# First attention's query and key products as matmul pairs over both halves of x, in two banks a panel

## The chip, the cores and the metric

The kernel runs on one core of one Trainium2 chip. The metric is the device time of one execution in microseconds; lower is better. All arithmetic is in fp32, with TensorE working on operands of type fp32r, so each large product is made of three: high half times high half, low times high, high times low.

## The reference

Two transformer blocks in a row work on `x` of 256 tokens by 1024. The first projects the normalised x to all its inputs at once, runs two mixers side by side, and adds a feed-forward network. The part that matters here is the first mixer, an attention with a forget gate:

```python
hn = rmsnorm(h, norm_mix[l])
proj = jnp.einsum('bsd,de->bse', hn, w_in[l])
(fq, fk, fv, ff, gq, gk, gv, ga, gb, gz, gate_fox, gate_gdn) = split_in(proj)
y_fox = fox_attention(fq.reshape(B, S, 8, 128), fk..., fv..., log_f)   # 8 heads
# in fox_attention, for each head and block of 128 queries:
s = jnp.einsum('bhqd,bhkd->bhqk', qi, kh) * 128 ** -0.5 + (ci[..., :, None] - c[..., None, :])
p = softmax(where(causal, s, -inf));  o = p @ vh
```

The other mixer is a chunked gated delta rule; in the stage of interest it needs the inverse of sixteen 128 x 128 lower triangular matrices. Then come gates, branch and output projections, the feed-forward networks, and the second block.

## The kernel before

**Steps.** All large products run as 252 steps, in one order written out in `panels()`. A panel is 1024 rows of a weight matrix by 256 columns (1 MB); a step multiplies half of one panel (`HALVES`), four rows-of-128 blocks `k`. `END[key]` is the last step of a product. Five programs run side by side, one for each engine, and each walks through `for n in range(1, STEPS + 1)` and does at step n what is written under it, strictly in that order. TensorE first does `gemm(n)`, then the small products of step n. ScalarE (`scalar_program`) and VectorE (`vector_program`) each begin step n with `split(n + 3)`: ScalarE rounds the raw panel to its high half (`panel_hi`, L1090, once TensorE has finished step n - 1), and VectorE subtracts it from the raw panel for the low half (`panel_lo`, L1586). SyncE fetches the panels (L2394) as VectorE sets raw buffers free.

**Forms of a product.** `gemm` (L584 is where every matmul is recorded) has three forms. "fm": weights are the stationary operand and 256 tokens of x stream by; three matmuls of 256 columns for each k and column tile j, and both column tiles lie in one bank of PSUM. "hl": the weights' high half meets both halves of x in one matmul of 512 columns, and their low half meets the high half of x in one of 256; a column tile then fills a whole bank, with high sums in columns 0 to 255 and low ones in 256 to 511, which are to be added afterwards. "wide": x is stationary. The convolution products (steps 5 to 32, but for z) and six of eight branch products are "hl" already. In the convolution stage they use three banks in turn (4, 0, 1), and the helpers' bank ring `side` is cut from four banks to three (5, 6, 7).

**Queries and keys.** Steps 41 to 56 make the first attention's queries and keys: panels fq0, fk0, fq1, fk1, ..., fk3, two steps each, in form "fm". Each fills one bank; `fox_project` on ScalarE, near the end of its program for the panel's last step, waits for that step's last matmul and copies the bank, scaled for queries, into two heads of `qfT` or `kfT`.

**What else runs at steps 40 to 60.** The attention takes one head every three steps: for head hh with F = 45 + 3 hh, TensorE makes the scores (L897 is the transpose, `fox_scores` uses `mm`) at the end of step F, VectorE adds the bias at F + 1 (L1830), ScalarE takes the exponential at F + 2 (L1259) and loads the next head's bias, VectorE normalises at F + 3 (L1838, L1841), and TensorE turns the tile at F + 4 (L897) and multiplies by the values at F + 5. Beside it VectorE inverts the diagonal 16 x 16 blocks row by row at steps 42 to 47 (L1757, L1760). SyncE writes the result to memory at step 48 (L2440, L2442) and reads it back into `X` and `XT` (L2448), which TensorE uses from the end of step 53 on. ScalarE zeroes `X` at step 42 and `XT` at step 44.

Of the kernel before, what the change touches and what calls it, by code (L numbers as in the profile page):

```python
# [23 lines left out]
P = 128  # L24
T = 256
# [66 lines left out]
def panels():  # L92
# [20 lines left out]
    for j in range(4):  # L113
        for kind, c0 in (("fq", C_FQ), ("fk", C_FK)):
            add((kind, j), "mix", True, "w_in", 0, KD, c0 + j * PW)
# [54 lines left out]
SQUARED_K = [c for c in SQUARED if CONVS[c][0] == "k"]  # L170
FOX_AT = {45 + 3 * hh: hh for hh in range(HEADS)}
# [31 lines left out]
def build(nc, a, out, scratch_a, scratch_x, scratch_c):  # L203
    ctx = ExitStack()
    with ctx:
# [29 lines left out]
        X = at("X", [P, UNITS, 64], 17)  # L235
        XT = at("XT", [P, UNITS, P], 18)
# [208 lines left out]
        s_yf_hi = sem("yf_hi")  # L445
        s_gate_f, s_gate_g, s_mixed, s_y_hi, s_y = (sem(n) for n in ("gate_f_affine", "gate_g_affine", "mixed", "y_hi",
# [18 lines left out]
        rings = {"few": [0, 1], "conv": [4, 0, 1], "fox": [2, 3], "side": [4, 5, 6, 7], "gemm": [0, 1, 2, 3]}  # L465
# [46 lines left out]
        def ring_of(key):  # L512
            if key[0] == "z" or key in (("fv", 0), ("fq", 0), ("fk", 0)):
                return "fox"
            if key in CONVS and CONVS.index(key) in CONV_BOTH:
                return "conv"
            return "few" if END[key] <= END["gate_g", 3] else "gemm"
# [64 lines left out]
        def tensor_program(e):  # L582
# [297 lines left out]
            def fox_scores(hh):  # L880
# [4 lines left out]
                e.wait_ge(*emptied(("fq", hh // 2)))  # L885
                e.wait_ge(*emptied(("fk", hh // 2)))
# [112 lines left out]
            for n in range(1, STEPS + 1):  # L999
# [3 lines left out]
                if n == END["v", 3] + 2:  # L1003
                    rings["side"] = [4, 5, 6, 7]
# [83 lines left out]
        def scalar_program(e):  # L1088
# [184 lines left out]
            def fox_project(kind, j):  # L1273
                e.wait_ge(*product((kind, j)))
                dst, scale = (qfT, float(DH) ** -0.5) if kind == "fq" else (kfT, 1.0)
                copy(dst[:, 2 * j:2 * j + 2, :], pairs(bank_of((kind, j))), scale).then_inc(empties((kind, j)), 1)
# [123 lines left out]
            for n in range(1, STEPS + 1):  # L1400
                split(n + 3)
                if n == 13:
# [99 lines left out]
                for j in range(4):  # L1502
                    for kind in ("fq", "fk"):
                        if n == END[kind, j]:
                            fox_project(kind, j)
# [72 lines left out]
        def vector_program(e):  # L1578
# [242 lines left out]

            def fox_bias(hh):
# [223 lines left out]
            for n in range(1, STEPS + 1):  # L2046
                split(n + 3)
                if n == 13:
# [135 lines left out]
                if n == 76:  # L2184
                    for b in range(4):
                        hi, lo = (y_[:, 2 * b:2 * b + 2, :].rearrange("p h (t q) -> p (h t) q", t=2)
                                  for y_ in (ygh, ygl))
                        e.wait_ge(s_yg_hi, b + 1)
                        e.scalar_tensor_tensor(lo, units(bank_of(("yg", b))), PR("gdn_norm"), hi.bitcast(F32), ALU.mult,
                                               ALU.subtract).then_inc(empties(("yg", b)), 1)  # L2190
                if n - 5 in FOX_AT:
# [362 lines left out]
```

## Time and profile before

| | us |
|---|---|
| median of 3 runs | 806.5 (806.42 to 807.1) |
| the profiled execution | 806.4 |
| its span | 805.1 |
| TensorE busy | 798.8 (99%) |
| VectorE busy | 599.7 (74%) |
| ScalarE busy | 451.0 (56%) |
| GpSimd busy | 73.8 (9%) |
| matmul instructions | 5448 |

Matmul records overlap, since they are pipelined: the time that one costs is the distance from its start to the start of the next. "PE" is TensorE, "PEld" its weight loads, "DVE" VectorE, "ACT" ScalarE, "POOL" GpSimd, "SPq" SyncE's queue. A few matmul records are missing in places, so distances are read from first to last start.

### The profile page before, as it was taken

What the parts mean: (1) busy time and instruction counts of PE and PEld (TensorE: products, weight loads), DVE (VectorE), ACT (ScalarE), POOL (GpSimd) and SP (SyncE); (2) the same over time, 40 slices, a digit from 0 to 9 for tenths busy, and PEclk for the clock granted to TensorE, in tenths of its full rate; (3) what the DMA queues carried; (4) which work ended last, traced back from release to release, by engine and by line L of the source; (5) the groups of instructions that cost most, each with busy time, mean ns of one, the idle gap of its engine ahead of it and who ended that gap; (6) DMA issues with size and microseconds to landing.
All of it is one profiled execution on the core that took longest, in us unless ns stands there. A gap on an engine that the chain in (4) does not pass through costs nothing.

```text
span 805.1 us, 13705 instructions
## 1 busy us (share of the span) xinstructions
PE 798.8 (99%) x5448; PEld 712.3 (88%) x5448; DVE 599.7 (74%) x1021; ACT 451.0 (56%) x739; POOL 73.8 (9%) x65
## 2 busy tenths in 40 slices
PE   8999999999999999999999999999999999999998
PEld 6888888999999989899999998887878888888887
DVE  6889998875554776769999996486766777778543
ACT  6667677454535554546656564366665655655441
POOL 0001000010011203001101110021100111011000
PEclk9999999999999999999999999999999999999999
DMA  8755564647442544575687665555425656656641
GB/s 262 239 173 160 179 229 148 173 108 223 125 116 90 178 162 161 204 242 179 198 248 244 213 204 194 178 183 171 144 82 168 203 177 208 191 177 207 191 154 73
DMA packets 126255, 144.12 MB, mean 179 GB/s; under 512 B 11488, under 2 KB 103024, under 8 KB 125936
## 3 DMA queue, kind: packets, MB, share of 16 engines
q1 hardware_dynamic: 123744, 141.22, 55.2%
q10 hardware_dynamic: 2448, 2.03, 0.9%
q8 instruction: 43, 0.70, 0.4%
q14 instruction: 20, 0.16, 0.1%
HBM read 141.78 MB, written 1.46 MB: 178 GB/s over the span
## 4 chain that ended last, share of the span: by engine, by line
PE 96%; DVE 2%; DMA 1%; ACT 0%; issue 0%; POOL 0%; SPq 0%; DVEq 0%; ACTq 0%
PE bank L584 93%; PE bank L638 1%; DMA panel_raw<-in_w_in 1%; DVE conv_acc L1622 1%; PE bank L948 0%; PE bank L670 0%; DVE panel_lo L1586 0%; PE bank L897 0%; PE bank L921 0%; PE bank L725 0%; DVE x_halves L1607 0%; POOL stats L2301 0%; ACT x_halves L1090 0%; DVE norm_gained L1881 0%; PE bank L827 0%
## 5 line engine op out<-in xcount | busy, mean ns | idle before, releaser
L584 PE MATMUL bank<-x_halves,panel_hi 128*128 128x256 f32 (+1 forms) x1792 | 415.1, 317 | 0.7 <-DVE x_halves L2032 0.7
L1586 DVE TENSOR_TENSOR panel_lo<-panel_raw,panel_hi 128x1024 fp32r<-128x1024 f32 x251 | 313.8, 1253 | 134.5 <-ACT panel_hi L1090 133.8
L1090 ACT ACTIVATE panel_hi<-panel_raw 128x1024 fp32r<-128x1024 f32 (+1 forms) x253 | 266.3, 1055 | 164.6 <-PE bank L584 160.4
L584 PE MATMUL bank<-x_halves,panel_lo 128*128 128x256 f32 x1152 | 324.4, 282 | 0.0
L584 PEld LDWEIGHTS bank<-x_halves,panel_hi 128*128 128x128 f32 x1792 | 295.8, 190 | 23.5 <-issue 0.9
L584 PEld LDWEIGHTS bank<-x_halves,panel_lo 128*128 128x128 f32 x1152 | 219.4, 190 | 0.2
L584 PE MATMUL bank<-panel_hi,x_halves 128*128 128x512 f32 x256 | 80.6, 396 | 0.2 <-DVE panel_lo L1586 0.2
L584 PE MATMUL bank<-panel_hi,act_hi 128*128 128x512 f32 x176 | 68.6, 390 | 0.0
L584 PE MATMUL bank<-panel_hi,act_lo 128*128 128x512 f32 x176 | 68.5, 389 | 0.0
L584 PE MATMUL bank<-panel_lo,act_hi 128*128 128x512 f32 x176 | 68.5, 389 | 0.0
L584 PEld LDWEIGHTS bank<-panel_hi,x_halves 128*128 128x128 f32 x256 | 46.7, 188 | 10.4 <-DVE panel_lo L1586 1.0
L584 PE MATMUL bank<-panel_lo,x_halves 128*128 128x512 f32 x128 | 50.0, 391 | 0.0
L584 PEld LDWEIGHTS bank<-panel_hi,act_hi 128*128 128x128 f32 x176 | 33.0, 188 | 6.9
L584 PEld LDWEIGHTS bank<-panel_lo,act_hi 128*128 128x128 f32 x176 | 33.0, 188 | 6.8
L584 PEld LDWEIGHTS bank<-panel_hi,act_lo 128*128 128x128 f32 x176 | 33.0, 188 | 6.7
L2301 POOL TENSOR_TENSOR stats<-stats 128x2 f32<-128x2 f32 (+1 forms) x9 | 17.1, 1899 | 183.9 <-DVE stats L1600 102.6
L1622 DVE SCALAR_TENSOR_TENSOR conv_acc<-conv_tmp,params,conv_acc 128x255 f32<-128x255 f32 (+2 forms) x72 | 30.4, 477 | 1.4 <-ACT conv_acc L1090 1.4
L584 PEld LDWEIGHTS bank<-panel_lo,x_halves 128*128 128x128 f32 x128 | 24.0, 188 | 5.3
L2326 POOL TENSOR_TENSOR ff_tanh<-ff_tanh,ff_val 128x512 f32<-128x512 f32 x11 | 17.2, 1564 | 112.4 <-DVE ff_tanh L1929 112.4
L2306 POOL TENSOR_TENSOR key_bias<-key_bias,constants 128x128 f32<-128x128 f32 x16 | 8.5, 550 | 176.9 <-DMA key_bias<-gate_sums 176.9
L2333 POOL TENSOR_TENSOR f_tanh<-f_tanh,ff_val 128x512 f32<-128x512 f32 x11 | 14.3, 1301 | 108.3 <-DVE f_tanh L2005 108.3
L584 PE MATMUL bank<-yf_halves,panel_hi 128*128 128x512 f32 (+1 forms) x80 | 22.7, 350 | 0.0
(291 smaller groups left out, 936.6 us busy)
## 6 DMA issues: line engine op xcount, KB each, us to landing
panel_raw<-in_w_in SPq DMA_DIRECT2D x38, 1024.0 KB, 5.3
panel_raw<-in_w_up SPq DMA_DIRECT2D x30, 1024.0 KB, 5.3
panel_raw<-in_w_down SPq DMA_DIRECT2D x20, 1024.0 KB, 5.1
panel_raw<-in_w_gate SPq DMA_DIRECT2D x10, 1024.0 KB, 5.3
panel_raw<-in_w_out SPq DMA_DIRECT2D x8, 1024.0 KB, 5.0
panel_raw<-in_w_in SPq DMA_DIRECT2D x11, 512.0 KB, 4.6
panel_raw<-in_w_branch_fox SPq DMA_DIRECT2D x4, 1024.0 KB, 5.1
panel_raw<-in_w_branch_gdn SPq DMA_DIRECT2D x4, 1024.0 KB, 5.3
```

The lines of the kernel that those rows point to most:

```text
L584: return e.matmul(o, l, r, start=start, stop=stop, skip_group_check=True)
L638: i_ = e.transpose(b3[:, k, m * P:(m + 1) * P], h[:, m, f * P:(f + 1) * P], ident)
L1090: return e.activation(o, i_, ACT.Copy, scale=scale)
L1586: e.tensor_tensor(lo, raw_view(i, k0, kt), hi.bitcast(F32), ALU.subtract).then_inc(s_lo, 1)
L1622: e.scalar_tensor_tensor(acc[:, f, back:], tmp[:, f, 0:T - back], gconv(p, f, back), acc[:, f, back:], ALU.mult, ALU.add).then_inc(s_taps, 1)
L2301: return e.tensor_tensor(cols, cols, minus_half.broadcast_to([P, n]), ALU.pow)
L2306: i_ = e.tensor_tensor(key_bias[:, s], key_bias[:, s], C("causal"), ALU.add)
L2326: e.tensor_tensor(th, th, ff_acc[j % 2][1], ALU.mult).then_inc(s_f_mul, 1)
L2333: e.tensor_tensor(th, th, ff_acc[j % 2][1], ALU.mult).then_inc(s_g_mul, 1)
```

## The change

The eight panels of queries and keys take the form "hl". They use the ring of three banks (4, 0, 1), two banks for each panel, and the side ring is cut to 5, 6, 7 from step 41 until step 58. ScalarE copies the low sums of both column tiles (256 columns each) to one of two new tiles at the front of its program for the panel's last step; the second copy waits for that step's last matmul. VectorE multiplies the high sums by the scale and adds the copy: for the first column tile at the front of its program for that step, for the second after that step's other duties, ahead of the attention's. `fox_project` is gone. `fox_scores` waits for the one tile that it reads.

```diff
-            add((kind, j), "mix", True, "w_in", 0, KD, c0 + j * PW)
+            out.append(((kind, j), "mix", "hl", "w_in", 0, KD, c0 + j * PW, PW))
...
+FQK = [(kind, j) for j in range(4) for kind in ("fq", "fk")]
...
+        fqk_low = [at(f"fqk_low{i}", [P, 2, T], 17.5, skip=2048 * i) for i in range(2)]
...
-        rings = {"few": [0, 1], "conv": [4, 0, 1], "fox": [2, 3], "side": [4, 5, 6, 7], "gemm": [0, 1, 2, 3]}
+        rings = {"few": [0, 1], "fqk": [4, 0, 1], "conv": [4, 0, 1], "fox": [2, 3], "side": [4, 5, 6, 7], "gemm": [0, 1, 2, 3]}
...
         def ring_of(key):
-            if key[0] == "z" or key in (("fv", 0), ("fq", 0), ("fk", 0)):
+            if key[0] == "z" or key == ("fv", 0):
                 return "fox"
+            if key in FQK:
+                return "fqk"
...
-                e.wait_ge(*emptied(("fq", hh // 2)))
-                e.wait_ge(*emptied(("fk", hh // 2)))
+                e.wait_ge(*emptied(("fq", hh // 2, hh % 2)))
+                e.wait_ge(*emptied(("fk", hh // 2, hh % 2)))
...
+                if n == FIRST_HALF["fq", 0] + 1:
+                    rings["side"] = [5, 6, 7]
+                if n == END["fk", 3] + 2:
+                    rings["side"] = [4, 5, 6, 7]
                 gemm(n)
...
-            def fox_project(kind, j):
-                e.wait_ge(*product((kind, j)))
-                dst, scale = (qfT, float(DH) ** -0.5) if kind == "fq" else (kfT, 1.0)
-                copy(dst[:, 2 * j:2 * j + 2, :], pairs(bank_of((kind, j))), scale).then_inc(empties((kind, j)), 1)
+            def fqk_low_copy(kind, j):
+                p = FQK.index((kind, j))
+                for m in range(2):
+                    if p >= 2:
+                        e.wait_ge(*emptied((*FQK[p - 2], m)))
+                    e.wait_ge(*product_of((kind, j), m))
+                    copy(fqk_low[p % 2][:, m, :], bank_of((kind, j, m))[:, T:2 * T],
+                         float(DH) ** -0.5 if kind == "fq" else 1.0).then_inc(s_fqk_low, 1)
...
             for n in range(1, STEPS + 1):
                 split(n + 3)
+                for kind, j in FQK:
+                    if n == END[kind, j]:
+                        fqk_low_copy(kind, j)
...
+            def fqk_sum(kind, j, m):
+                p = FQK.index((kind, j))
+                dst, scale = (qfT, float(DH) ** -0.5) if kind == "fq" else (kfT, 1.0)
+                e.wait_ge(s_fqk_low, 2 * p + m + 1)
+                e.scalar_tensor_tensor(dst[:, 2 * j + m, :], bank_of((kind, j, m))[:, 0:T], scale,
+                                       fqk_low[p % 2][:, m, :], ALU.mult, ALU.add).then_inc(empties((kind, j, m)), 1)
...
             for n in range(1, STEPS + 1):
                 split(n + 3)
+                for kind, j in FQK:
+                    if n == END[kind, j]:
+                        fqk_sum(kind, j, 0)
...
+                for kind, j in FQK:
+                    if n == END[kind, j]:
+                        fqk_sum(kind, j, 1)
                 if n - 5 in FOX_AT:
                     fox_lo(FOX_AT[n - 5])
```

## Rows read from the trace of the kernel before

**Rows 1.** The page: busy us (share) xinstructions; tenths in 40 slices; the chain's shares.

```profile
PE 798.8 (99%) x5448; PEld 712.3 (88%) x5448; DVE 599.7 (74%) x1021; ACT 451.0 (56%) x739; POOL 73.8 (9%) x65
...
DVE  6889998875554776769999996486766777778543
...
PEclk9999999999999999999999999999999999999999
...
PE 96%; DVE 2%; DMA 1%; ACT 0%; issue 0%; POOL 0%; SPq 0%; DVEq 0%; ACTq 0%
```

**Rows 2.** The chain that ended last, 125 to 290 us, by line.

```profile
by line: PE bank L584 96.4%; PE bank L897 1.8%; PE bank L725 1.1%; PE bank L827 0.6%; PE bank L670 0.3%
```

**Rows 3.** Timeline of TensorE: start us, us, line, op, out<-in, size, count.

```profile
142.53 0.48 PE L584 MATMUL bank<-x_halves,panel_hi 128*128 128x256 f32 x2
...
157.01 0.82 PE L584 MATMUL bank<-kfT,qfT 128*128 128x128 f32 x4
...
169.82 0.49 PE L897 MATMUL bank<-constants,fox_p 128*128 128x128 f32 x3
...
183.39 2.06 PE L584 MATMUL bank<-X,BT 64*64 64x32 f32 x64
```

**Rows 4.** Timeline of TensorE, first and last of 15 and of 29 pairs.

```profile
74.34 0.39 PE L584 MATMUL bank<-x_halves,panel_hi 128*128 128x512 f32 x1
...
79.63 0.40 PE L584 MATMUL bank<-x_halves,panel_hi 128*128 128x512 f32 x1
...
299.79 0.39 PE L584 MATMUL bank<-yg_halves,panel_hi 128*128 128x512 f32 x1
...
309.84 0.39 PE L584 MATMUL bank<-yg_halves,panel_hi 128*128 128x512 f32 x1
```

**Rows 5.** Timeline of VectorE, end of step 40.

```profile
141.92 0.69 DVE L1744 TENSOR_TENSOR decayT<-bank,decayT 128x512 f32<-128x512 f32 x1 [0.20 <-PE bank L584]
...
143.42 1.28 DVE L2205 COPY vf<-bank 128x512 f32<-128x512 f32 x2
```

**Rows 6.** Timeline of VectorE, steps 45 to 48; in brackets idle before, releaser.

```profile
155.90 1.22 DVE L1586 TENSOR_TENSOR panel_lo<-panel_raw,panel_hi 128x1024 fp32r<-128x1024 f32 x1 [0.63 <-ACT panel_hi L1090]
...
158.92 1.22 DVE L1586 TENSOR_TENSOR panel_lo<-panel_raw,panel_hi 128x1024 fp32r<-128x1024 f32 x1
...
165.53 1.21 DVE L1586 TENSOR_TENSOR panel_lo<-panel_raw,panel_hi 128x1024 fp32r<-128x1024 f32 x1
...
168.06 0.55 DVE L1841 TENSOR_SCALAR fox_p<-fox_p,stats 128x128 f32<-128x128 f32 x2
```

**Rows 7.** Timeline of ScalarE, steps 42 to 45.

```profile
148.56 0.60 ACT L1090 ACTIVATE qfT<-bank 128x512 f32<-128x512 f32 x1 [0.81 <-PE bank L584]
...
152.47 1.90 ACT L1090 ACTIVATE XT<-constants 128x2048 f32<-128x2048 f32 x1
...
154.82 1.05 ACT L1090 ACTIVATE panel_hi<-panel_raw 128x1024 fp32r<-128x1024 f32 x1
```

**Rows 8.** Groups of instructions, whole span: busy us, mean ns | idle before, releaser.

```profile
L1607 DVE SCALAR_TENSOR_TENSOR x_halves<-bank,params,x_halves 128x256 fp32r<-128x256 f32 x28 | 11.6, 476 | 2.2 <-ACT x_halves L1090 2.0
...
L1630 DVE TENSOR_TENSOR conv_tmp<-bank,conv_tmp 128x256 f32<-128x256 f32 x20 | 7.7, 417 | 2.0 <-ACT conv_tmp L1090 2.0
```

**Rows 9.** Timeline of VectorE, two sums of a branch product back to back.

```profile
310.88 0.75 DVE L1860 TENSOR_TENSOR branch_low<-bank,branch_low 128x256 f32<-128x256 f32 x2
```

**Rows 10.** Groups of instructions: TensorE's weight loads of the products out of x.

```profile
L584 PEld LDWEIGHTS bank<-x_halves,panel_hi 128*128 128x128 f32 x1792 | 295.8, 190 | 23.5 <-issue 0.9 <-DVE conv_tmp L1630 0.6 <-DVE panel_lo L1586 0.2
```

**Rows 11.** Timeline of SyncE's queue, step 48: when it issues.

```profile
165.22 0.34 SPq L2440 DMA_DIRECT2D blocks_inverted<-blocks_X  x1
...
173.72 3.77 SPq L2448 DMA_DIRECT2D X<-blocks_inverted  x8
```

**Rows 12.** DMA issues of 140 to 200 us: count, KB each, median us to landing.

```profile
blocks_inverted<-blocks_X SPq DMA_DIRECT2D x1, 128.0 KB, 8.4
...
X<-blocks_inverted SPq DMA_DIRECT2D x8, 16.0 KB, 3.0
```

## What the change should do to the time

> **What bounds the kernel now.** I read the page's engine shares and its chain first: TensorE is busy for 99% of the span and the chain of work that ended last lies on it for 96%, at a granted clock of nine tenths or more in every slice [rows 1]. So a change pays only by what it takes out of TensorE's stream, and costs only what makes that stream wait. The chain through the stage that is changed is a run of matmuls alone [rows 2]: nothing waits there today. The rates of the stream come from TensorE's timeline. Steps 41 to 45 (the first five of the sixteen that are changed, 41 to 56) run from 142.53 to 157.01 us: 120 matmuls of 256 columns, 121 ns each, so 0.36 us for one triple and 2.89 us for a step [rows 3]. The same timeline elsewhere has the form that comes in its place, a 512-column matmul and a 256-column one. In the convolution products 15 such pairs take 5.29 us, 0.353 us each; in the second branch product 29 take 10.05 us, 0.347 us each [rows 4]. Last I read what TensorE's helpers do here, because the edit gives them work. VectorE has no idle time between 155.90 and 168.61 us, after 0.63 us of it just before [rows 6]: its chain (low halves of the panels, the rows of the 16x16 inversion, the first head's softmax) is what the stage is nearly short of.
>
> **Part 1, the matmuls.** Each of 8 panels has 16 (k, column tile) places; 128 triples become 128 pairs. The columns that stream stay the same (768 per place); what goes is one matmul and one weight load. Gain per place: 0.360 - 0.353 = 0.007 us or 0.360 - 0.347 = 0.013 us [rows 3, 4], in all 0.9 to 1.7 us. I take 0.010, the middle, since both rows are of the same form and I see no reason in them for the difference: 1.3 us, or 0.08 us for a step (2.80 us in place of 2.88).
>
> By the Trainium skill (TensorE: Matmul & The Clock Gate, Back-to-back issue gap) an isolated matmul costs N/2.4 + 2.5 ns, so a triple would be 327.5 and a pair 325.0 ns, and the part would bring about 0.3 us (an estimate from that page). The rows differ from it in both forms, by 33 ns and by 22 to 28 ns, and they decide; that the form as such brings next to nothing is kept as a rival below.
>
> **Part 2, banks.** A panel now fills two banks, of a ring of three (4, 0, 1), and the other products keep 5 to 7 from step 41 to 57. The first tile of step 41 goes to bank 4, which held the third of the four q-k products; VectorE leaves it at 141.92 + 0.69 = 142.61 us, while TensorE would start at 142.53 [rows 3, 5]. That is a wait of 0.1 to 0.2 us. The second goes to bank 0, whose value tile is copied out at 143.42 + 0.64 = 144.06 [rows 5], when it is wanted at about 144.1: none. With three banks, the second tile of panel p+1 takes the bank of the first tile of panel p. It is wanted half a step (1.4 us) after panel p ends, and is free only when VectorE has summed. The pairs of small products from step 53 on find a bank whose last reader they await anyway: nothing.
>
> **Part 3, ScalarE.** It loses one copy of 512 columns per panel, late in its program for the step, and gets two copies of 256 columns at the step's front. The second waits for the step's last matmul, and queued behind it are all of ScalarE's duties of that step. In step 44 this is the zeroing of XT (1.85 us), which today comes before the copy and runs while TensorE multiplies [rows 7]. After the change: step 44 ends at 142.7 + 4 x 2.80 = 153.9; the copy starts 0.2 us later (as that of step 42 does, at 148.56, two steps after 142.53 being 148.3) and takes 0.3, half of today's 0.60; the zeroing ends at 156.3 and the high half of step 48's panel at 157.3, 1.4 us later than today's 155.9 [rows 7]. VectorE, which waits for that high half today too (its 0.63 us of idle time before 155.90 [rows 6]), starts at 157.35 in place of 155.90. VectorE's own queue would be free at 155.27 plus the four earlier sums, 156.9, so it is not far behind as a limit.
>
> **Part 4, VectorE.** It gets two sums of 256 columns out of PSUM per panel. Such an instruction in this place is not in the trace. The nearest are the scale-and-subtract out of PSUM with 0.476 us, the convolution's sum with 0.417 [rows 8], and 0.75 - 0.42 = 0.33 us from one to the next where two sums stand back to back [rows 9]. I take 0.41, since the new ones are single and wait for a semaphore each. From 155.90 to the end of the first head's normalisation (168.06 + 0.55 = 168.61) is 12.7 us of work without idle time [rows 6]. Four sums (steps 46 and 48) come into it: 12.7 + 4 x 0.41 = 14.35 us, which ends at 157.35 + 14.35 = 171.7 us.
>
> **Who is late next.** TensorE turns that first head after step 49, at 169.82 us today [rows 3], 1.2 us after it is ready. Without waits it would come there at 169.82 + 0.15 - 9 x 0.08 = 169.2. Now it can't start before 171.8. On the way it waits twice for a bank. In step 47 the sum of the first tile of step 46 ends at about 157.35 + 3.02 + 1.14 + 0.41 = 161.9, wanted at 161.5 (the low half of step 49 starts 158.92 - 155.90 = 3.02 us into VectorE's chain, that of step 51 at 165.53 - 155.90 = 9.63 [rows 6]). In step 49 that of step 48 ends at 157.35 + 9.63 + 0.82 + 1.14 + 0.41 = 169.35, wanted at 168.2. After that the second half of step 49 ends at 170.85, and the turn waits the remaining 0.9 us. These waits of 0.4, 1.1 and 0.9 us lie in one another's chain and are not to be added to the end that VectorE sets.
>
> **Sum.** At the turn TensorE is 171.8 - 169.8 = 2.0 us late, the gain of nine steps already in it. From there VectorE and ScalarE have idle time enough, and seven steps win 0.08 us each: 2.0 - 0.56 = +1.4 us. The profiled execution took 806.4 us (span 805.1, about 1.3 around it), so it would be 807.8; the median of the runs is 0.1 above it, so **807.9 us**. With the sum at 0.33 or 0.48 us, the pair at 0.347 or 0.353, and 0.2 to 0.3 us of doubt in where ScalarE frees the high half, this case spans 807.0 to 808.7. Small stalls like these leave the clock alone, I think: today's rows show no slice below nine tenths, the start of the kernel with its waits among them [rows 1].
>
> **The rivals.**
> First, the sums hide and the gain stays. The convolution stage runs this very scheme (same ring, the first tile summed within the panel's last step) with VectorE at nine tenths in some slices, and TensorE's weight loads waited for its sums for 0.6 us in the whole kernel, over 20 tiles [rows 1, 10]. Scaled to 16 tiles that is 0.5 us. If VectorE's chain has more give than I read, say because the zeroing does not hold up the high half, the time is 806.5 - 1.3 + 0.15 + 0.5 = 805.8, and with the pair at 0.347 and no wait at all 806.5 - 1.7 = 804.8. Against it: between 155.90 and 168.61 there is no idle time to hide 1.64 us in, and only 1.2 us of slack ahead of the turn, less than the 1.4 us of the late high half alone.
> Second, slower: the inverse comes late. VectorE's last inversion row moves from 165.2 to about 167.5 us. SyncE waits for it to write the blocks out, waits 8.4 us until they land, and only then loads them into X, the loads landing about 3 us after their issue [rows 11, 12]; no panel is fetched meanwhile. Today X is whole at 177.5 + 3.0 = 180.5 and wanted at 183.39 [rows 3]. After: 182.8 against 185.4 - 0.3 = 185.1. It decides from 2.3 us of further delay. A write of 12 us, for instance, makes the first block product wait 1.3 us and gives 809.2.
> Third, the change does not do what it says: a pair takes as long as a triple, as where something other than the count of matmuls sets the pace. Against it, both rows of pairs [rows 4]. Then step 44 ends 0.3 us later, the turn comes at 172.1, 2.3 us late, and nothing is won back: 808.8. This is also where the skill's gap rule leads.
>
> **How the numbers follow.** Forecast 0.50, the first rival 0.27, the second 0.13, the third 0.05, and 0.05 for something unseen. A measurement of this kernel can tell 0.2%, 1.6 us, from no change: under 804.9 is faster, over 808.1 slower. Faster holds only the end of the first rival, 0.06. Within: most of the first rival (0.22) and 0.35 of the forecast's 0.50 (its point is 807.9, and 808.1 lies just above it), with a little unseen, 0.58. Slower: the rest of the forecast, both last rivals, 0.36. The range reaches from most of the first rival, 805.2, to most of the second, 809.0. The forecast's own is 807.0 to 808.7.
>
> **What would show it.** In the timeline of after, a pair of 0.347 to 0.353 us in steps 41 to 56 (part 1). VectorE's low half of step 48 starting at about 157.4 with ScalarE's zeroing of XT right before its high half (part 3). No idle time on VectorE from there to about 171.7 (part 4). The chain of waits passing from TensorE to VectorE's sums or softmax at 160 to 172 us, and the first turn at about 171.8 against 169.82. After it, steps of 2.80 to 2.83 us where there were 2.88, and the same distances from gate products to the end. What would make it wrong: the turn at 169.3 with no waits (first rival), a second stop at the block products near 185 us (second), or a turn later than 172.5, if exponentials or the sums queue worse than I lined them up.

## The result, and the profile after

The changed kernel takes 807.6 us (median of 18 runs, 807.3 to 808.9), the kernel before 806.6 us on the same chip (18 runs, 806.2 to 807.2): a ratio of 1.0014, 95% interval 1.0007 to 1.002, so 1.06 us or 0.13% slower. The forecast was 807.9, in a range of 805.2 to 809.0. The difference lies inside the 0.2% that the forecast called no change. One thing has to be known for the medians further down: some executions of every kernel, before's among them, have a mean granted clock of 0.947 to 0.998 and take mostly 1.2 to 2.3 us longer (0.6 to 3.2 at the ends), and two, at clocks of 0.74 and 0.75, took 996 and 980 us and stand in the medians alone.

The page of after (busy time by engine, TensorE's granted clock by slice, shares of the chain that ended last), to be read against [rows 1]:

```profile
PE 798.3 (99%) x5320; PEld 705.1 (87%) x5320; DVE 605.2 (75%) x1037; ACT 451.9 (56%) x747; POOL 74.3 (9%) x65
...
PEclk9999999999999999999999999999999999999999
...
PE 93%; DVE 4%; DMA 2%; ACT 1%; issue 1%; SPq 0%; DVEq 0%; ACTq 0%
```

There are 128 matmuls fewer and 16 instructions more on VectorE, and 3% of the chain has left TensorE. The chain, in order of time (start us, us, what), shows where it went; in [rows 2] this stretch was TensorE alone:

```profile
139.84 15.85 PE bank L589 x100
...
156.00 1.91 ACT XT L1100
157.90 0.95 ACT panel_hi L1100
...
158.88 1.23 DVE panel_lo L1601
...
170.29 0.42 DVE kfT L1841
170.71 1.13 DVE qT L2158
...
172.56 0.36 DVE fox_p L1863
...
173.05 0.52 PE bank L902 x3
173.57 9.74 PE bank L589 x58
```

It leaves TensorE at the end of step 44, passes ScalarE's zeroing of XT and its late high half, runs through 14 us of VectorE without a pause, and comes back at the turn of the first head. This is the path of Parts 3 and 4.

**Three landmarks** compare the kernels, all starts on TensorE: the first q-k product (q-k; the change begins right behind these products), the first turn, which transposes the first head's softmax tile (L897 before, L902 after), and the first matmul of the last group of block products of the inversion (32x32, at step 57). Stretches between them are free of what the start of the kernel does. That matters, since the profiled execution of after took 808.8 us and its q-k was already 1.54 us late, before anything that was changed:

```profile
139.04 3.73 PE L584 MATMUL bank<-qT,kT 128*128 128x128 f32 x32
...
204.15 0.54 PE L584 MATMUL bank<-XT,PX 32*32 32x32 f32 x22
```

is before (TensorE's timeline: start us, us, line, op, out<-in, size, count), and

```profile
140.58 3.73 PE L589 MATMUL bank<-qT,kT 128*128 128x128 f32 x32
...
173.05 0.52 PE L902 MATMUL bank<-constants,fox_p 128*128 128x128 f32 x3 [0.61 <-DVE fox_p L1863]
...
186.35 2.06 PE L589 MATMUL bank<-X,BT 64*64 64x32 f32 x64
...
206.92 0.76 PE L589 MATMUL bank<-XT,PX 32*32 32x32 f32 x36
```

is after. The stage from q-k to the last block product is 204.15 - 139.04 = 65.11 us before and 206.92 - 140.58 = 66.34 after: **+1.23 us**. From q-k to the turn it is 169.82 - 139.04 = 30.78 [rows 3] and 32.47: +1.69. The rest is won back behind the turn (-0.46). The 1.54 us of the start belong to this one execution: TensorE stood idle there at 25.86 us for 0.90 us until ScalarE was done (`conv_acc`), in the convolution's first steps, while experiment 1, the same kernel up to step 43, has its q-k at 138.94.

**One more difference lies far outside the change.** From the second mixer's first output turn (285 us) to the end, after is 0.36 us shorter (519.18 against 519.54). A weight load of the second block waits for a low half, 0.65 us in before and 0.28 in after:

```profile
544.53 0.19 PEld L584 LDWEIGHTS bank<-panel_hi,x_halves 128*128 128x128 f32 x1 [0.65 <-DVE panel_lo L1586]
```

```profile
546.99 0.30 PEld L589 LDWEIGHTS bank<-panel_hi,x_halves 128*128 128x128 f32 x2 [0.28 <-DVE panel_lo L1601]
```

The low half stands behind a row of small operations on `stats`. In VectorE's timeline one of them starts 0.46 us after the end of the one before it in before, and 0.10 us after it in after:

```profile
540.10 0.09 DVE L1592 DVE_READ_ACCUMULATOR2_ANT stats<- 128x1 f32 x1
540.64 0.16 DVE L1598 TENSOR_REDUCE stats<-stats 128x4 f32<-128x8 f32 x1 [0.46 <-DVE stats L1592]
```

```profile
542.91 0.08 DVE L1607 DVE_READ_ACCUMULATOR2_ANT stats<- 128x1 f32 x1
543.09 0.16 DVE L1613 TENSOR_REDUCE stats<-stats 128x4 f32<-128x8 f32 x1
```

All fourteen traces of this study show one of the two: five have 0.46 us here, 0.64 to 0.65 at the weight load and a tail of about 519.6, nine have 0.10, 0.28 to 0.30 and about 519.2. Three kernels with pairs (4, 5, 10 below) have the long tail and two without (7, 11) the short one, so it is no merit of the pairs. Why the reduction starts at once or 0.35 us later is open. Stage and tail together give 1.23 - 0.36 = +0.87 us for the changed kernel; the medians say +1.06.

### The profile page after: what moved, and what is told of

It is laid out like the page before. It is cut to its first block, busy times and chain, and to the rows that moved or that the text cites. A ratio compares the mean times of both kernels' runs of the same rounds, so it can differ in the third digit from the quotient of the medians.

```text
span 807.5 us, 13485 instructions
## 1 busy us (share of the span) xinstructions
PE 798.3 (99%) x5320; PEld 705.1 (87%) x5320; DVE 605.2 (75%) x1037; ACT 451.9 (56%) x747; POOL 74.3 (9%) x65
## 4 chain that ended last, share of the span: by engine, by line
PE 93%; DVE 4%; DMA 2%; ACT 1%; issue 1%; SPq 0%; DVEq 0%; ACTq 0%
PE bank L589 90%; DMA panel_raw<-in_w_in 2%; DVE panel_lo L1601 1%; DVE conv_acc L1637 1%; PE bank L643 1%; PE bank L953 0%; PE bank L675 0%; ACT panel_hi L1100 0%; PE bank L902 0%; DVE blocks_T L1772 0%; PE bank L926 0%; ACT XT L1100 0%; DVE blocks_X L1775 0%; PE bank L730 0%; ACT x_halves L1100 0%
## 5 line engine op out<-in xcount | busy, mean ns | idle before, releaser
L589 PEld LDWEIGHTS bank<-x_halves,panel_hi 128*128 128x128 f32 x1664 | 279.7, 190 | 31.3 <-ACT conv_acc L1100 1.2
```

The costliest lines, as they stand in the source:

```text
L589: return e.matmul(o, l, r, start=start, stop=stop, skip_group_check=True)
```

## The experiments

Each was timed beside the kernel before, in 11 or 12 executions (7 in five). All times in us. "Turn" is from q-k to the first turn, "stage" from q-k to the last block product, "tail" from 285 us to the end. The column "clock 1.0" is the median of the executions at a mean granted clock of 1.000, and the one to compare (before's was 806.42 to 806.69 in the four jobs).

| kernel | median | before, same job | clock 1.0 | turn | stage | tail |
|---|---|---|---|---|---|---|
| before | 806.56 | | 806.5 | 30.78 | 65.11 | 519.54 |
| after | 807.62 | 806.56 | 807.57 | 32.47 | 66.34 | 519.18 |
| 1 XT later | 806.71 | 806.71 | 806.50 | 31.66 | 65.53 | 519.23 |
| 2 four banks | 808.65 | 806.71 | 807.88 | 32.63 | 66.96 | 519.15 |
| 3 late panels | 806.13 | 806.71 | 806.11 | 30.69 | 64.93 | 519.15 |
| 4 no sums | 806.70 | 806.71 | 806.58 | 31.31 | 65.19 | 519.61 |
| 5 GpSimd sums | 806.64 | 806.59 | 806.57 | 31.15 | 65.03 | 519.65 |
| 6 chain cut | 805.85 | 806.59 | 805.85 | 30.90 | 64.99 | 519.19 |
| 7 delay alone | 810.09 | 806.59 | 809.48 | 33.48 | 67.84 | 519.17 |
| 8 moves alone | 806.69 | 806.60 | 806.63 | 30.78 | 65.11 | 519.57 |
| 9 no bank waits | 809.15 | 806.60 | 808.01 | 32.44 | 66.79 | 519.15 |
| 10 pairs alone | 809.18 | 806.60 | 807.78 | 32.37 | 66.21 | 519.65 |
| 11 half delay | 806.67 | 806.60 | 806.13 | 30.78 | 65.10 | 519.21 |
| 12 early sum | 805.84 | 806.61 | 805.83 | 30.55 | 64.92 | 519.15 |

806.5 plus a kernel's differences in stage and tail gives its "clock 1.0" within 0.25 us in every row but one (7: 808.9 by this sum, 809.48 from two runs). So stage and tail hold what the kernels differ by; the tail has two values that no edit here was meant to change, and what an edit did is read from the stage.

### 1. The zeroing of XT one step later

```diff
-                if n == 44:
+                if n == 45:
                     e.wait_ge(*filled(("qk", 3)))
```

> The changed kernel with one move: ScalarE zeroes XT at step 45 in place of step 44, so that it no longer stands between the second low copy of step 44 and the high half of step 48. My theory (the end is set by a chain from TensorE's step 44 over ScalarE's copy, zeroing and high half to VectorE's work up to the first head's normalisation): the high half comes 1.9 us earlier, VectorE's own queue is free 0.78 us before today's start, so the low half of step 48 and the first turn come 0.8 us earlier. From the first q-k product to the first turn 31.7 us in place of 32.5 (before the change 30.8), and the time about 806.8. Rival 1 (the ring of three banks costs the time): part of the wait of step 49 goes, the turn as early as that, no sharper forecast. Rival 2 (the sums alone cost it, wherever they start): 807.6, nothing moves.

Turn 31.66, time 806.7; TensorE's only listed wait between 125 and 290 us is 0.6 us at the turn. One of ScalarE's duties, moved one step, takes 0.81 us off the stage. The late high half of Part 3 is real and was about half of the 1.69 us at the turn.

### 2. Four banks in place of three

```diff
-                    rings["side"] = [5, 6, 7]
+                    rings["side"], rings["fqk"] = [6, 7], [4, 0, 1, 5]
+                if n == FIRST_HALF["fq", 2] + 1:
+                    rings["side"], rings["fqk"], ring_at["fqk"] = [5, 6, 7], [4, 0, 1], 0
```

> The changed kernel with a ring of four banks (4, 0, 1, 5) for the first four panels, steps 41 to 48, where no small product needs bank 5; from step 49 on the ring of three. My theory: the bank waits of steps 47 (0.3 us) and 49 (0.9 us) go and the wait for the first turn grows by as much, from 0.8 to 2.0 us, since VectorE's chain sets it. First q-k product to first turn 32.5 us as now, the time 807.6 within 0.1. Rival 1 (the ring costs the time): 1.2 us less, 806.4, with the turn at 31.3.

The waits for banks are gone, and the turn is where it was, at 32.63; the time, 807.88 at clock 1.0, misses the forecast by 0.3. In TensorE's timeline of after the stage had two of them:

```profile
163.51 0.50 PE L589 MATMUL bank<-x_halves,panel_hi 128*128 128x512 f32 x1 [0.17 <-DVE qfT L1841]
...
170.76 0.50 PE L589 MATMUL bank<-x_halves,panel_hi 128*128 128x512 f32 x1 [0.77 <-DVE kfT L1841]
```

With four banks there is one wait:

```profile
172.45 0.52 PE L902 MATMUL bank<-constants,fox_p 128*128 128x128 f32 x3 [1.94 <-DVE fox_p L1865]
```

Steps 46 to 49 take 2.07 us more here than in experiment 10, which has no wait in them, and 2.15 us more in after, so the one wait costs as much as the three of after together. The rival that the ring of three is the cost falls: its waits lie in the shadow of the end that VectorE sets. The stage is even 0.6 us longer than after's. Of this the turn has 0.2 (steps 41 to 45 take 14.23 us for 13.99, and VectorE's chain begins 0.17 us later), and 0.38 is a late start of the first gate product at step 57, which experiment 3 explains.

### 3. Pairs only in the last four panels (steps 49 to 56)

```diff
+            out.append(((kind, j), "mix", "hl" if j >= 2 else "fm", "w_in", 0, KD, c0 + j * PW, PW))
...
+FQK = [(kind, j) for j in range(2, 4) for kind in ("fq", "fk")]
...
```

> The new form for the last four panels alone (steps 49 to 56); the first four keep three matmuls of 256 columns and ScalarE's one copy. My theory: the new form costs only where VectorE has no idle time. So no wait for a bank, the first turn at 30.8 us after the first q-k product as before the change, and eight steps of 2.80 in place of 2.88: about 0.6 us under the kernel before, 806.0 (805.8 to 806.2). Rival 3 (a pair is no shorter than a triple): 806.6. If the sums and the three banks cost by themselves: above 806.6.

The time is 806.1 us, the turn 30.69, and no wait of TensorE is listed from 125 to 290 us. Up to the last value product (199.97 us) the 64 pairs bring 0.56 us, 9 ns each, which is the 0.6 of the forecast, and no sum costs anything on the way. But the stage is only 0.18 us shorter, since the last sum costs 0.38 us at step 57. VectorE and TensorE there:

```profile
200.47 0.42 DVE L1850 SCALAR_TENSOR_TENSOR kfT<-bank,fqk_low 128x256 f32<-128x256 f32 x1
```

```profile
199.97 0.94 PE L589 MATMUL bank<-fox_pT,vf 128*128 128x128 f32 x6
201.04 0.47 PE L589 MATMUL bank<-x_halves,panel_hi 128*128 128x256 f32 x2
```

With eight tiles in the ring 4, 0, 1 the last one lies in bank 0, which the rings of the kernel give to the first gate product; that starts 1.07 us after the value product, in before 0.69. In experiment 2 the last tile lies in bank 0 too; with the sixteen tiles of after it lies in bank 4, and the distance is 0.69. So 806.1 for a forecast of 806.0 is in part luck: the lost 0.38 us is made up by the short tail. What the run shows is that all of the loss at the turn belongs to steps 46 to 49.

### 4. No sums

```diff
...
-                    copy(fqk_low[p % 2][:, m, :], bank_of((kind, j, m))[:, T:2 * T],
-                         float(DH) ** -0.5 if kind == "fq" else 1.0).then_inc(s_fqk_low, 1)
+                    copy((qfT if kind == "fq" else kfT)[:, 2 * j + m, :], bank_of((kind, j, m))[:, 0:T],
+                         float(DH) ** -0.5 if kind == "fq" else 1.0).then_inc(empties((kind, j, m)), 1)
...
-                        fqk_sum(kind, j, 0)
...
-                        fqk_sum(kind, j, 1)
```

> The changed kernel without VectorE's eight pairs of sums: ScalarE copies the high sums straight to the heads and frees the bank, at the same places; the low sums (weights' high half times x's low half) are left out of queries and keys, so its output is not the reference's. My theory: ScalarE is as late as now with the high half of step 48, but four sums of 0.34 us go from the chain behind it. First q-k product to first turn 31.1 us in place of 32.5, the time 1.4 us less, 806.3; no bank waits. If only ScalarE's delay counted: 807.6 with the turn where it is. If the gain of the pairs were eaten elsewhere: near 807.

The turn is 31.31 and the time 806.7, a miss by 0.2 and 0.4 us; 0.4 us of the time is the long tail that this kernel has. There is still a wait of 0.6 us at the turn: the high half of step 48 is late with the sums gone too, since the zeroing of XT alone moves VectorE's start. The run prices the sums besides. VectorE's chain begins and ends here with

```profile
157.78 1.23 DVE L1599 TENSOR_TENSOR panel_lo<-panel_raw,panel_hi 128x1024 fp32r<-128x1024 f32 x1 [1.54 <-ACT panel_hi L1100]
...
169.93 0.55 DVE L1861 TENSOR_SCALAR fox_p<-fox_p,stats 128x128 f32<-128x128 f32 x2
```

which is 12.70 us, as before [rows 6], and 14.02 in after: 1.32 for four sums. The miss of 0.2 us at the turn is where the chain begins, 18.47 us after q-k in place of 18.30, since the pairs of steps 41 to 45 take 14.22 us here and 13.99 in after.

### 5. The sums on GpSimd

```diff
...
+                            e.tensor_tensor(d, d, fqk_low[FQK.index((kind, j)) % 2][:, m, :],
+                                            ALU.add).then_inc(s_fqk_sum, 1)
...
```

> The changed kernel with all sums taken from VectorE: ScalarE copies the low and the high sums out (two copies of 256 columns for each column tile, the second tile's at the old place late in the step), which frees the bank, and GpSimd adds them in SBUF; XT is zeroed at step 45. The computation is complete. My theory: VectorE's chain is back to 12.7 us, its start at most 0.5 us late, nothing waits for a bank, so the first turn comes as TensorE reaches it, 30.2 us after the first q-k product (before the change 30.8, now 32.5), and the gain of all sixteen steps stays: 805.6 (805.2 to 806.0), 1 us under the kernel before. If GpSimd's adds slow VectorE beside them, or the pairs bring nothing: 806.5 or more.

This was a clear miss: turn 31.15 for 30.2, time 806.6 for 805.6. GpSimd's timeline and VectorE's in the same stretch:

```profile
155.10 1.20 POOL L2381 TENSOR_TENSOR kfT<-kfT,fqk_low 128x256 f32<-128x256 f32 x1 [3.42 <-ACT kfT L1099]
156.51 0.74 POOL L2381 TENSOR_TENSOR kfT<-kfT,fqk_low 128x256 f32<-128x256 f32 x1 [0.21 <-ACT kfT L1099]
```

```profile
155.61 0.77 DVE L1776 TENSOR_TENSOR blocks_T<-blocks_X,blocks_A 128x36 f32<-128x36 f32 x1
...
156.63 0.72 DVE L1776 TENSOR_TENSOR blocks_T<-blocks_X,blocks_A 128x49 f32<-128x49 f32 x1
...
157.63 0.27 DVE L1776 TENSOR_TENSOR blocks_T<-blocks_X,blocks_A 128x64 f32<-128x64 f32 x1
```

In after the same two multiplications take 0.22 and 0.25 us:

```profile
156.24 0.22 DVE L1772 TENSOR_TENSOR blocks_T<-blocks_X,blocks_A 128x36 f32<-128x36 f32 x1
...
156.72 0.25 DVE L1772 TENSOR_TENSOR blocks_T<-blocks_X,blocks_A 128x49 f32<-128x49 f32 x1
```

Each met a GpSimd addition, took 0.5 us more, and ended 0.1 us after it (156.38 and 157.35 against 155.10 + 1.20 = 156.30 and 156.51 + 0.74 = 157.25). The third, which met none, has its usual length. GpSimd was held as well: its first addition met a low half of VectorE that had begun before it (154.48 us) and took 1.20 us in place of 0.74. So the work taken from VectorE (0.33 us a sum) comes back as a wait (0.5 us). The Trainium skill (SBUF — State Buffer, Who interferes with whom) says that an instruction of VectorE with two inputs in SBUF contends with one of GpSimd that reads SBUF, and that they share a port pair under a lock, so that the later one stands still until the other is done. The trace agrees: the multiplications, with two inputs, end with GpSimd's addition, and a reduction, with one, is not held. This one lies wholly within an addition (162.87 to 163.79 us) and took 0.31 us, in after 0.30:

```profile
163.20 0.31 DVE L1779 TENSOR_REDUCE blocks_X<-blocks_T 128x12 f32<-128x144 f32 x1
```

### 6. The chain cut in three places

```diff
-                if n == 44:
+                if n == 45:
                     e.wait_ge(*filled(("qk", 3)))
...
-                if n == 49:
+                if n == 50:
                     e.wait_ge(s_qdec, 1)
...
-                if n == 48:
+                if n == 49:
                     e.wait_ge(s_gc_exp, 1)
```

The first is ScalarE's zeroing of XT, the second its zeroing of PX, the third VectorE's multiplication of `qT`.

> The changed kernel with XT zeroed at step 45 and with VectorE's multiplication of qT (1.2 us), which stands between the sums and the first head's normalisation at step 48, moved to step 49, where VectorE waits for a key bias anyway; ScalarE's zeroing of PX, which waits for it, moves to step 50. No work goes away. My theory (a chain on VectorE up to the normalisation): the 0.8 us that the turn still waits with XT moved alone go, 0.3 us for the bank in step 49 stay. First q-k product to first turn 30.9, the time 0.8 under that kernel: 805.9. If the sums and the bank ring cost time as such, wherever the chain ends: 806.7, as with XT moved alone.

Both numbers came as expected, 805.85 and 30.90. The ratio to before is 0.999 with an interval of 0.998 to 0.9999: 0.7 us faster than before (0.6 at clock 1.0) and 1.8 faster than after. But against before the stage gives only 0.12 us of this and the tail 0.35, which is luck. TensorE still starts late by 0.23 us at the first bank, 0.36 in step 49 and 0.2 at the first value product. With the 1.13 us of `qT` out of the way, VectorE ends the normalisation 30.34 us after q-k (32.32 in after).

### 7. The delay without the change

```diff
...
+                if n == 42:
+                    e.memset(spare[0], 0.0).then_inc(s_spare, 1)
+                if n in (46, 48):
+                    for i in range(4):
+                        e.wait_ge(s_spare, 1 + i + 2 * (n - 46))
+                        e.scalar_tensor_tensor(spare[1], spare[0], 1.0, spare[0], ALU.mult, ALU.add).then_inc(s_spare, 1)
```

> The kernel before, form of the products unchanged, with eight idle sums of 256 columns put into VectorE's program, four at the front of step 46 and four at that of step 48, between spare tiles. It prices the cover. My theory: eight times 0.40 us less the 1.2 us by which the normalisation is ready ahead of the turn: the first turn 2.0 us later, 32.7 us after the first q-k product in place of 30.8, one wait of 2.0 us there and no other, time 808.5 (808.0 to 808.9). If TensorE does not depend on VectorE there: 806.6.

Expected 808.5 and turn 32.7, measured 810.1 (809.5 at clock 1.0) and 33.48. VectorE's timeline prices one such sum at 0.45 us in place of 0.33; each waits for the one before, and none reads PSUM, and which of the two makes the difference was not tried:

```profile
160.54 1.79 DVE L2054 SCALAR_TENSOR_TENSOR spare<-spare 128x256 f32<-128x256 f32 x4
...
168.85 1.80 DVE L2054 SCALAR_TENSOR_TENSOR spare<-spare 128x256 f32<-128x256 f32 x4
...
172.23 0.63 DVE L1842 TENSOR_SCALAR fox_p<-fox_p,stats 128x128 f32<-128x128 f32 x2
```

The end of the normalisation moved by 3.75 us and the turn by 2.70: the cover ahead of the turn is 1.05 us, and beyond it each microsecond on VectorE is one of TensorE. The mechanism holds without a single pair in the kernel.

### 8. The moves of experiment 6 in the kernel before

> The kernel before with the three moved duties of the cut-chain kernel alone (zeroing of XT to step 45, multiplication of qT on VectorE to step 49, zeroing of PX to step 50), no pair. It asks whether that kernel's 805.85 us is owed to the pairs or to the moves. Before, TensorE waits for nothing in steps 41 to 56, so by the theory the moves free nothing: the first turn stays 30.8 us after the first q-k product, the stage to the last block product 65.1, the time 806.6 us, give or take 0.2. The rival is that the moves themselves bring the time down, in the stage or behind it: then 805.9 us or so, and the pairs are worth nothing even with the waits gone.

Turn 30.78, stage 65.11, 806.6 us, all three as before. The normalisation ends 1.2 us sooner (28.38 us after q-k for 29.58), and nobody wants it sooner. So the moves pay only in the changed kernel, where they undo its cost.

### 9. Both remaining waits for banks attacked

Against the kernel of experiment 6:

```diff
-        rings = {"few": [0, 1], "fqk": [4, 0, 1], "conv": [4, 0, 1], "fox": [2, 3], "side": [4, 5, 6, 7], "gemm": [0, 1, 2, 3]}
+        rings = {"few": [0, 1], "fqk": [1, 4, 0], "conv": [4, 0, 1], "fox": [2, 3], "side": [4, 5, 6, 7], "gemm": [0, 1, 2, 3]}
...
+                if n == END["fk", 1]:
+                    fqk_sum("fk", 1, 0)
                 split(n + 3)
...
```

> The cut-chain kernel, with its two remaining waits for a bank attacked: the ring starts with bank 1 (free since a step) in place of bank 4, and VectorE takes the sum of the first tile of step 48 ahead of a panel's low half in place of behind it. In the cut-chain kernel these waits showed as 0.22 us at the first q-k stretch (3.71 against 3.49 us) and 0.38 us in step 49. Without them the turn would be 30.90 - 0.22 - 0.38 = 30.3 us after the first q-k product, but VectorE ends the normalisation at 30.3, so it comes at 30.5. Expected: turn 30.5, stage 64.6 us, time 805.85 - 0.4 = 805.4 us. The rival, that the bank waits are only the outer sign of TensorE running ahead and something else holds it as soon as they go, gives turn 30.9 and 805.8 us again.

The forecast was wrong: 808.0 at clock 1.0, turn 32.44. I had read that bank 1 was free at step 41. It holds the second tile of the last value panel, which VectorE copies out last. In TensorE's timeline of this kernel:

```profile
144.93 0.47 PE L589 MATMUL bank<-x_halves,panel_hi 128*128 128x512 f32 x1 [2.07 <-DVE vf L2235]
```

The order 4, 0, 1 of the change is the right one: it asks for the banks as they come free.

### 10. Pairs alone

Experiment 4 with the zeroing of XT at step 45 and the ring of experiment 9.

> The changed kernel without its sums (the low halves of queries and keys are left out), with the zeroing of XT a step later and the ring starting at bank 1: pairs alone, with nothing left to wait for. It prices part 1 by itself. From the distances in the kernels already run (14.48 to 14.22 us in steps 41 to 45, 8.82 to 8.67 in 46 to 48, 3.06 to 2.97 in 49, then 0.46 up to the last block product): turn 30.3 us after the first q-k product, stage 64.2, time 806.6 - 0.95 = 805.65 us. By the prediction's 0.010 us per place it would be 805.3. The rival that a pair takes as long as a triple gives 806.6 us, stage 65.1.

The time of 805.65 was missed, with 807.8 at clock 1.0: the ring cost it the same stop, 2.07 us of idle time; the stretch of the q-k products is 5.80 us for 3.49, so 2.31 us in all. The rest still prices Part 1, with nothing else to wait for: the stage is 66.21 - 2.31 = 63.90 us against 65.11, a gain of **1.21 us**, or 9.5 ns for each of 128 places. In the table by stretches (us, then each engine's busy time and instructions, clock, DMA) steps 41 to 45 take, in before and here:

```profile
142.53:157.01 14.48, 14.48 (x124) 14.48 (x123) 12.61 (x30) 7.92 (x8) 0.00 (x0) 1.00 0.52 157
```

```profile
145.00:158.94 13.94, 13.94 (x80) 12.29 (x81) 10.14 (x26) 7.74 (x10) 0.00 (x0) 1.00 0.52 161
```

The rival that a pair takes as long as a triple is dead. This subtraction of a stop is arithmetic on one trace, not a run of its own; the 0.56 us for 64 places of experiment 3, whose kernel leaves nothing out, agree with it.

### 11. Two added sums in place of eight

Against the kernel of experiment 7:

```diff
-                if n in (46, 48):
-                    for i in range(4):
+                if n == 46:
+                    for i in range(2):
```

> The kernel before with two additional sums of 256 columns on VectorE at the front of step 46, in place of eight in steps 46 and 48. Measured in the kernel with eight: 0.43 us each, and 1.05 us of cover ahead of the first turn. Two are 0.87 us, under the cover: the turn stays at 30.8 us after the first q-k product, with the normalisation ending at 30.45, and the time at 806.6 us. The rival, that every microsecond given to VectorE in this stretch arrives at the end, gives turn 31.65 and 807.5 us.

The normalisation ends 0.78 us later (30.36 us after q-k) and the turn stays at 30.78. Beneath the cover VectorE's time is free, as forecast. At clock 1.0 this kernel is even 0.4 us faster than before, nearly all of it in the tail (519.21), with an unchanged stage (65.10): the tail's third of a microsecond comes and goes without a pair.

### 12. The early sum alone

The edit of experiment 9 on VectorE, with the ring 4, 0, 1.

> The cut-chain kernel with one more move: VectorE takes the sum of the first tile of step 48 ahead of a panel's low half in place of behind it, so that its bank is free when step 49 asks for it; the ring stays bank 4, 0, 1, since bank 1 turned out to hold a value tile until VectorE has copied it. In the cut-chain kernel this bank made the middle of step 49 0.38 us longer. Expected: step 49 of 3.0 us in place of 3.37, the first turn 30.90 - 0.38 = 30.5 us after the first q-k product (VectorE ends the normalisation at 30.3 and allows just that), stage 64.6 us, time 805.85 - 0.4 = 805.45 us. The rival, that the low half which the sum is put ahead of then comes late for TensorE or the turn takes up the wait, gives turn 30.9 and 805.8 us.

The turn came at 30.55, as expected, and the next wait took the gain: the stage is 64.92, not 64.6, and the time 805.8 as in experiment 6. TensorE and VectorE in this kernel:

```profile
173.19 0.94 PE L589 MATMUL bank<-fox_pT,vf 128*128 128x128 f32 x6 [0.25 <-DVE stats L1852]
```

```profile
172.50 0.29 DVE L1852 CUSTOM_DVE_ANT_0 fox_p<-bank,key_bias 128x128 f32<-128x128 f32 x1 [0.42 <-POOL key_bias L2336]
```

What is late now is the second head's scores, which VectorE reads only when GpSimd has the key bias ready. In experiment 6 this already held the value product back by 0.2 us.

## Why the prediction was right, step by step

**Part 1, the pairs: right, with the point at the upper end.** Forecast 1.3 us (0.9 to 1.7), measured 1.21 in experiment 10. The other kernels can be read against its stretches. In after the late starts add up to 2.38 us (0.23 at the first bank, 0.36 in steps 46 to 48, 1.79 from there to the turn) and the stage is 1.23 us longer, so the pairs brought 1.15 us; the same reckoning gives 0.92 to 0.95 in experiments 1, 4, 5, 6 and 12. The difference is one of pace. The two of [rows 4] both occur in the stage: steps 41 to 45 take 13.94 to 13.99 us in after, 9 and 10 (0.3467 a pair in after from 146.50 to 157.94 us, 33 pairs) and 14.21 to 14.23 in the others (0.353). Experiment 1 and after have the same program there, so the pace is not set by the edit, and taking the middle was as much as the rows allowed.

**Part 2, the first bank: right.** Forecast 0.1 to 0.2 us; the stretch of q-k products is 3.72 us in after for 3.49, so 0.23.

**Part 3, ScalarE: right.** The zeroing of XT stands ahead of the high half of step 48, and VectorE's low half starts late:

```profile
155.71 0.39 ACT L1100 ACTIVATE fqk_low<-bank 128x256 f32<-128x256 f32 x1 [1.00 <-PE bank L589]
156.00 1.91 ACT L1100 ACTIVATE XT<-constants 128x2048 f32<-128x2048 f32 x1
```

```profile
158.88 1.23 DVE L1601 TENSOR_TENSOR panel_lo<-panel_raw,panel_hi 128x1024 fp32r<-128x1024 f32 x1 [0.78 <-ACT panel_hi L1100]
```

158.88 less the 1.54 us of this execution's start is 157.34; the forecast said 157.35, against 155.90 before [rows 6]. That it fits to 0.01 us is luck: with the slower pace of pairs (experiments 2 and 4) the same instruction starts 18.47 us after q-k, in after 18.30.

**Part 4, VectorE: the mechanism right, a term too large.** There is no idle time from 158.88 on, and four sums lie in it, as forecast. Each adds 0.33 to 0.34 us to the chain, not 0.41:

```profile
163.04 0.42 DVE L1841 SCALAR_TENSOR_TENSOR qfT<-bank,fqk_low 128x256 f32<-128x256 f32 x1
163.38 0.39 DVE L1772 TENSOR_TENSOR blocks_T<-blocks_X,blocks_A 128x144 f32<-128x144 f32 x1
...
172.35 0.55 DVE L1863 TENSOR_SCALAR fox_p<-fox_p,stats 128x128 f32<-128x128 f32 x2
```

The record is 0.42 us, but the next instruction starts 0.34 after it. [Rows 9] had said so, and I took nearly the length of a record for the reason that the sums are single; in a chain that never idles they overlap their neighbours like all the rest. The chain took 172.90 - 158.88 = 14.02 us for a forecast 14.35. That is the 0.3 us by which the turn came too early for my sum: +1.69 measured, +2.0 forecast.

**The waits: right in kind.** The middle of step 47 and of step 49 and the turn each start late, by 0.33, 0.94 and 0.77 us as distances of starts (0.4, 1.1 and 0.9 forecast), and experiment 2 shows that they are one another's shadow. Behind the turn 0.46 us came back, 0.56 forecast. The stage is thus +1.23 for +1.4, and the tail, of which the forecast knew nothing, takes 0.36 off. By these two the time would have come 0.5 us under the forecast; by the medians it is 0.3, and the other 0.2 us are not resolved. So the mechanism and the stage were forecast, and the tail's share in the total is luck.

**The rivals.** The first (the sums hide) holds for steps 49 to 56, but for 0.38 us at their end where the last tile lies in bank 0 (experiment 3), and below a cover of 1.05 us (experiments 7 and 11), and fails in steps 46 to 49. The second (a late inverse) did not occur: from the turn to the first block product, after takes 13.30 us and before 13.57. The third is excluded by experiment 10.

**What stays open.** How the two paces of one stream of pairs come about; why VectorE's reduction in the tail starts at once or 0.35 us later; and why experiment 7 is 0.6 us longer than its stage and tail say, on two runs (one is the profiled execution, and its q-k came 0.49 us later than before's).

## What to carry to other kernels

A change that saves TensorE instructions by giving work to the helpers is worth what the helper's slack is at that place: here VectorE's bill was 2.7 us (1.4 from a duty queued behind a new wait, 1.3 from four sums), of which 1.05 us were covered. TensorE came 1.69 us late to the turn, whatever the pairs had saved up to there, and only the 0.46 us that they saved behind it counted. Before adding a wait at the front of an in-order engine, look at what stands behind it and whether that could stand a step later; three such moves turned a stage of +1.23 us into one of -0.12 (and the medians from +1.1 to -0.7, a part of which is the tail). And take the cost of an instruction in a busy chain from the distance to its neighbour, not from the length of its record.

## What the runs showed of the hardware

**A GpSimd addition and a VectorE operation on two tiles stop each other.** A 128x256 addition on GpSimd (0.74 us alone) beside VectorE made multiplications of 0.22 and 0.25 us last 0.77 and 0.72, and itself took 1.20 us where VectorE had begun first (experiment 5); a reduction within an addition kept its 0.3 us. An operation on one tile was held as well: the 128x256 multiplication of `blocks_A` took 0.83 us beside an addition and 0.28 in after.

**A row of small operations on VectorE has two lengths.** One reduction of 128x8 starts 0.10 or 0.46 us after an accumulator read, in nine and five of fourteen traces, and the end of the kernel moves with it by 0.3 to 0.5 us (tails of 519.15 to 519.23 and 519.54 to 519.65).

**One stop of about 2 us and the clock.** The kernels in which TensorE stops once for 1.9 to 2.5 us (2, 7, 9, 10) had a mean granted clock below 1 in 20 of 38 runs, the other experiments and after in 15 of 105, before in 13 of 104. That is most of why their medians lie above the column "clock 1.0". In which stretch the clock falls in those runs is open, since their profiled executions all had 1.000. One profile caught a fall elsewhere: in experiment 5 the granted clock is 0.58 in the first stretch of dense matmuls, that is at the lower level of 1.2 GHz for most of it, behind 5.70 us (5.00 to 10.70) of which TensorE was busy for 3.46, in before for 4.18. Where before has 23 matmuls this stretch has 15, and q-k comes 1.37 us later than before's (us, busy time and count for each engine, clock, DMA, of that kernel, then of before):

```profile
10.70:13.50 2.80, 2.79 (x15) 2.80 (x16) 2.49 (x6) 2.80 (x5) 0.00 (x0) 0.58 0.41 131
```

```profile
10.80:13.60 2.80, 2.79 (x23) 2.80 (x24) 2.49 (x6) 2.80 (x6) 0.00 (x0) 1.00 0.42 133
```
